# Page attention of a decoder step: the values of four cache pages in one part, directly behind the scores

## The chip, the cores and the metric

The kernel runs on one core of a Trainium2 chip. The metric is the device time of one execution in microseconds (us); lower is better. TensorE does the matrix products and the transpositions, VectorE (DVE) and ScalarE (ACT) copy out of PSUM and do the softmax; GpSimd (POOL), SyncE (SP) and ScalarE issue DMAs. Everything is float32.

## The reference, cut to what matters

One layer of a hybrid decoder is computed for a prompt of 1024 tokens and for 8 samples of 8 new tokens each. The change lies in the attention of the samples over their paged cache: 2048 past tokens in 16 pages of 128 rows, found through a page table, 8 heads of 64.

```
kv_past = cache_fox_kv[page_table, l].reshape(Bd, P, 2, N_FOX_HEADS, HEAD_DIM)
...
k_all = jnp.concatenate([kv_past[:, :, 0], k_new], axis=1)
v_all = jnp.concatenate([kv_past[:, :, 1], v_new], axis=1)
s = jnp.einsum('bqhd,bkhd->bhqk', q, k_all) * (dh ** -0.5)
s = s + c_q.transpose(0, 2, 1)[..., None] - c.transpose(0, 2, 1)[:, :, None, :]
s = jnp.where(mask, s, -inf)
p = softmax(s)
return jnp.einsum('bhqk,bkhd->bqhd', p, v_all)
```

`c` is the running sum of log forget values. After it comes a second page attention of the samples over three dilated windows (13 pages of 128 picked rows, 4 heads each), then gates, projections, a cross-attention and an MLP.

## The kernel before, in words

Each engine has one instruction stream, and its order is written out by `weave`: several generators yield due times (not microseconds), and the one that is due first goes on. `PLAN` holds the stages' due times: the page attention `fox=(869, 1223)`, the gate products `ga=(715, 1010)` and `gb=(1010, 1448)`, `dilprep=(1226, 1228)`, the dilated pages `dil=(1230, 1422)`. On TensorE the page work is woven with the gate products of the prompt (`gates_pe`, L1867 and L1875). A gate unit has 8 + 4 k steps of 352 or 368 columns in the first pass and 8 + 2 in the second; each pass has 24 units. A k step is one product, two matmul records in the trace.

`paged` makes the list of steps for all three page attentions. For the paged cache ("fox") the steps of a sample b are:

- T: the four 128 x 128 transpositions of a page of keys (L1289) into one of two PSUM banks. ScalarE copies out the even pages (L1355), VectorE the odd ones (L1348); page n waits until page n - 2 is copied out.
- S: the scores of a group of four pages, four head pairs in four column tiles of 16 columns (L1305), one slot behind the page that completes the group. One more group, for the 8 new keys, comes one slot behind the sample's first page. VectorE drains each group with the bias added and its maximum taken (L1385).
- M: the maximum over the groups on VectorE (L1390) and one exponential over the row on ScalarE (L1360). TensorE does nothing at M.
- P: transpositions of the probabilities in five blocks (L1314), each copied out to `PT_f` by VectorE (L1400).
- V: the values, 17 blocks in 16 parts of one page each (the last one with the new values), four column tiles again (L1325). They add up in one PSUM bank.
- O: the result scaled (L1407), transposed (L1332) and copied.

Slot i of a sample holds its T of page i; P and V of sample b lie in the slots of sample b + 1, at the offsets in `fox_tail`. All steps of the list get due times in equal steps over `fox`; before, the list has 352 steps.

The pages come by DMA, 256 KB for the keys and 256 KB for the values of one. SyncE loads the keys into four slots (`foxk_sp`, L1500), each when its old page is transposed. ScalarE loads the values into five slots (`foxv_page_act`: page number read at L1514, DMA issued at L1515), each when the part of the page five before is done, in its one stream with its copies. GpSimd spreads the bias rows of each score group with four DMAs (`foxbias_pool`, L1532) into one of two buffers, when this many drains are done:

```
pool.wait_ge(*nth(pg_fox, "drained", bb * 5 + 2 + GG))
```

`dilprep_sp` (L1712) loads a table and then the new dilated keys `kn_d`, 24 DMAs of 8 KB on SyncE's queue (L1721), at a quarter of the `fox` stage. `dilk_sp` and `dilv_sp` load the dilated keys and values. `dilpages_dve` clears `vn_d` and then copies the transposed new keys (L1805, L1809).

## Time and profile before

| | |
|---|---|
| time, median of 3 runs (lowest, highest) | 2754.54 us (2754.12, 2763.18) |
| span of the profiled execution, first to last instruction | 2753.4 us |
| around the span, taken from the median | 1.1 us |
| TensorE matmuls busy | 2717.2 us, 99% |
| VectorE, ScalarE, GpSimd busy | 42%, 19%, 5% |
| mean granted TensorE clock | 0.998 of full |
| HBM traffic | 268.07 MB read, 63.35 MB written, 120 GB/s over the span |
| the page stage on TensorE | about 839 to 1182 us |
| the dilated pages | about 1186 to 1345 us |

The profiled execution's time itself is its span and what lies around it; it is compared with the median of the runs above. Printed durations of matmuls overlap each other: what one takes of TensorE is the difference from its start to the next start. "PEld" is the loading of weights, which lies beside the matmuls. A queue's row such as "SPq" tells from the first issue to the end of the last one.

### The profile page before, as it was taken

How to read it: one execution, taken by the hardware profiler on the slowest of the kernel's cores; microseconds unless marked ns; L12 is line 12 of the kernel's file. 1: busy time of each engine (PE TensorE's matmuls, PEld its weight loads, DVE VectorE, ACT ScalarE, POOL GpSimd, SP SyncE). 2: the span in 40 equal slices, each digit the busy share in tenths (PEclk: the TensorE clock that was granted, in tenths of full speed). 3: DMA queues.
4: the chain of work that ended last, by engine and by line, in shares of the span. 5: the costliest groups of instructions: out<-in, count | busy, mean ns of one | idle time of the engine just before them, and what ended most of it. 6: DMA issues, size and time to landing. Idle time of an engine off the chain costs nothing.

```text
span 2753.4 us, 37659 instructions
## 1 busy us (share of the span) xinstructions
PE 2717.2 (99%) x14274; PEld 1846.9 (67%) x14274; DVE 1151.5 (42%) x2788; ACT 528.6 (19%) x1163; POOL 145.4 (5%) x268
## 2 busy tenths in 40 slices
PE   8999999999999999999999999999999999999998
PEld 7655556767655555456644577546888888888887
DVE  2255543332253233333264023345666666654432
ACT  2233322221201112111002122231212211210002
POOL 1000001020101122100000000000000000000000
PEclk9999999999999999999999999999999999999999
DMA  5000102000116779866512300434435433152201
GB/s 190 22 13 9 59 20 67 32 17 20 46 27 185 210 220 266 248 187 196 217 51 78 136 31 31 147 115 125 146 113 186 145 110 126 46 179 86 80 29 65
DMA packets 207160, 294.48 MB, mean 107 GB/s; under 512 B 20781, under 2 KB 145086, under 8 KB 205942
## 3 DMA queue, kind: packets, MB, share of 16 engines
q1 hardware_dynamic: 148150, 187.76, 21.1%
q10 hardware_dynamic: 42976, 89.26, 10.2%
q0 software_dynamic: 15856, 15.07, 2.3%
q8 instruction: 115, 1.88, 0.3%
q14 instruction: 63, 0.52, 0.1%
HBM read 268.07 MB, written 63.35 MB: 120 GB/s over the span
## 4 chain that ended last, share of the span: by engine, by line
PE 96%; DMA 1%; DVE 1%; issue 1%; SPq 0%; ACTq 0%; ACT 0%; DVEq 0%
PE psum L2523 21%; PE psum L955 11%; PE psum L2904 10%; PE psum L1867 9%; PE psum L531 5%; PE psum L2207 4%; PE psum L1953 4%; PE psum L1289 4%; PE psum L702 3%; PE psum L2054 3%; PE psum L1875 3%; PE psum L718 3%; PE psum L1325 3%; PE psum L1305 2%; PE psum L2181 2%; PE psum L729 2%
## 5 line engine op out<-in xcount | busy, mean ns | idle before, releaser
L2523 PE MATMUL psum<-arena 128*128 128x272 f32 x2464 | 566.6, 393 | 1.2 <-DVE arena L2597 1.2
L2523 PEld LDWEIGHTS psum<-arena 128*128 128x128 f32 x2464 | 469.1, 190 | 98.0 <-issue 1.3
L955 PE MATMUL psum<-arena 128*128 128x512 f32 (+3 forms) x960 | 316.8, 481 | 0.0
L1867 PE MATMUL psum<-arena 128*128 128x368 f32 (+1 forms) x768 | 299.4, 490 | 1.2 <-DVE arena L1809 1.2
L2904 PE MATMUL psum<-arena 128*128 128x256 f32 (+1 forms) x1584 | 288.1, 356 | 0.0
L2904 PEld LDWEIGHTS psum<-arena 128*128 128x128 f32 (+1 forms) x1584 | 252.5, 178 | 34.6 <-issue 3.2
L955 PEld LDWEIGHTS psum<-arena 128*128 128x128 f32 (+1 forms) x960 | 195.0, 250 | 60.7 <-issue 35.1
L778 DVE CUSTOM_DVE_ANT_0 arena<-psum,arena 128x256 f32<-128x256 f32 (+2 forms) x224 | 95.4, 457 | 207.7 <-PE psum L702 207.3
L1867 PEld LDWEIGHTS psum<-arena 128*128 128x128 f32 x768 | 123.7, 191 | 68.5 <-issue 42.9
L2626 DVE TENSOR_TENSOR arena<-arena,psum 128x272 f32<-128x272 f32 (+2 forms) x330 | 111.8, 378 | 112.8 <-PE psum L2523 112.0
L752 ACT ACTIVATE arena<-arena 128x256 f32<-128x256 f32 (+4 forms) x192 | 107.5, 562 | 227.0 <-DVE arena L778 225.5
L1289 PEld LDWEIGHTS psum<-arena 128*128 128x128 f32 x848 | 102.9, 142 | 65.5 <-issue 42.6
L1348 DVE COPY arena<-psum 128x512 f32<-128x512 f32 (+1 forms) x108 | 73.6, 682 | 168.3 <-PE psum L1289 168.2
L531 PE MATMUL psum<-arena 128*128 128x288 f32 (+1 forms) x384 | 137.6, 482 | 0.0
L2647 DVE SCALAR_TENSOR_TENSOR arena<-arena 128x1024 f32<-128x1024 f32 x88 | 113.1, 1285 | 52.6 <-ACT arena L2549 51.1
L1355 ACT ACTIVATE arena<-psum 128x512 f32<-128x512 f32 (+1 forms) x108 | 63.6, 589 | 369.5 <-PE psum L1289 352.3
L1289 PE MATMUL psum<-arena 128*128 128x128 f32 x848 | 130.8, 277 | 3.4 <-DMA arena<-in_cache_fox_kv 3.2
L2547 ACT ACTIVATE arena<-arena 128x1024 f32<-128x1024 f32 x44 | 54.2, 1233 | 399.9 <-DVE arena L2626 399.9
L1953 PE MATMUL psum<-arena 128*128 128x512 f32 x256 | 123.5, 599 | 0.0
L2207 PE MATMUL psum<-arena 128*128 128x288 f32 (+1 forms) x384 | 122.6, 468 | 0.0
L3016 DVE TENSOR_TENSOR arena<-arena,psum 128x256 f32<-128x256 f32 (+1 forms) x128 | 46.6, 401 | 178.9 <-PE psum L2904 178.8
L788 DVE COPY arena<-psum 128x128 f32<-128x128 f32 (+1 forms) x96 | 37.6, 391 | 191.7 <-PE psum L718 191.5
(245 smaller groups left out, 2953.6 us busy)
## 6 DMA issues: line engine op xcount, KB each, us to landing
arena<-in_cache_fox_kv ACTq DMA_DIRECT2D x128, 256.0 KB, 4.2
arena<-in_cache_fox_kv SPq DMA_DIRECT2D x128, 256.0 KB, 4.3
out_win_s<-in_cache_win_kv ACTq DMA_DIRECT2D x8, 4080.0 KB, 15.5
arena<-in_w_up SPq DMA_DIRECT2D x44, 512.0 KB, 6.4
arena<-in_w_down SPq DMA_DIRECT2D x14, 1408.0 KB, 6.3
arena<-in_cache_win_kv SPq DMA_DIRECT2D x16, 1024.0 KB, 7.8
arena<-in_cache_mem_kv SPq DMA_DIRECT2D x16, 1024.0 KB, 6.4
arena<-in_w_in SPq DMA_DIRECT2D x9, 1024.0 KB, 7.8
```

Source lines behind the costliest of these rows:

```text
L531: last = pe.matmul(banks[q % 2][:, 0:cw], w[:, k, j * P:(j + 1) * P], xnT[:, k, c0:c0 + cw], start=(k == 0), stop=(k == KD - 1))
L752: act.activation(p, p, ACT.Exp, scale=-1.0, bias=a["NM"][i], accum_out=a["L"][i]).then_inc(s["expd"], 1)
L778: dve.tensor_tensor_reduce(a["Pb"][i % 4][:, c0:c1], SCORE[h][:, 0:c1 - c0], un["add"](h)[:, c0:c1], 1.0, a["GM"][:, i % 4:i % 4 + 1] if c ...
L955: last = pe.matmul(banks[c0 // 512][p0:p0 + r, 0:n], xn_tile(k, g, t), wD[g][:, k, w0:w0 + n], start=(k == 0), stop=(k == KD - 1))
L1289: last = pe.transpose(a["turn"][n % 2][:, x * P:(x + 1) * P], k, ident)
L1867: last = pe.matmul(banks[0][:, 0:cw], w[:, k, :], xnT[:, k, c0:c0 + cw], start=(k == 0), stop=(k == KD - 1))
L1953: last = pe.matmul(banks[h], lhs(k)[:, t * P:(t + 1) * P], w[h][:, k, :], start=(k == 0), stop=(k == KD - 1))
L2207: last = pe.matmul(banks[u % 2][:, 0:cw], wX[n % 2][:, k, (m % 4) * P:(m % 4 + 1) * P], xnT[:, k, c0:c0 + cw], start=(k == 0), stop=(k == ...
L2523: last = pe.matmul(bank_of(j, x, p), w[:, k, :], r[:, k, Q4 * p:Q4 * p + Q4], start=(k == 0), stop=(k == 3))
L2626: last = dve.tensor_tensor(dst, dst if base is None else view(base), view(bank), ALU.add)
L2647: dve.scalar_tensor_tensor(out=tp, in0=up[:, tap:tap + S], scalar=w, in1=tp, op0=ALU.mult, op1=ALU.add).then_inc(done, 1)
L2904: last = pe.matmul(down_out(u)[p0:p0 + r, 0:n], hT(f)[:, tok + t * P:tok + t * P + r], slot[slots[c]][:, f - fa, c0:c0 + n], start=(f == f ...
```

## The change

Values are taken in four parts of four pages (the last with the new values too), each placed in the slot of a score group and ahead of the other tail work of that slot. On TensorE a score group and a value part that follow each other in the list no longer yield between them, and M is left out of TensorE's list; this holds for all three page attentions. The score group of the new keys moves from behind the first page to behind the last (`new_at`), so it is drained last. The list has 256 steps for the same due span. Values get seven slots instead of five, with one semaphore for every other part; ScalarE loads the pages of a slot when the part that used it is done. The two new slots take the place of `kn_d` and of part of its neighbours; `kn_d` moves onto the first score buffer, so its 24 loads wait until the last probability block of sample 6 is transposed, and `vn_d`, which now overlaps it, is cleared behind the copy of the new keys.

```
--- before.py
+++ after.py
@@ -1212,7 +1212,7 @@
 
 
         def paged(turns, groups, R, kts, s_sb, p_blocks, p_keep, pv, v_split, o_sb, o_blocks, stats, take_out, tail_at, due,
-                  banks_of, add_ready=None, made=False):
+                  banks_of, add_ready=None, made=False, new_at=0):
 
             nt, gl = len(turns(0)), groups(0, None)
             drains = [x for x, g in enumerate(gl) if g["drain"] is not None]
@@ -1239,7 +1239,7 @@
                 sched += [(kind, bb, q) for slot, bb, _, kind, q in tails if slot == n]
                 if b < NB:
                     scores += [("S", b, x) for x in range(len(gl))
-                               if gl[x]["turned"] == i + 1 or (i == 0 and gl[x]["turned"] is None)]
+                               if gl[x]["turned"] == i + 1 or (i == new_at and gl[x]["turned"] is None)]
                     if i == nt - 1:
                         scores.append(("M", b, 0))
             assert not scores
@@ -1277,9 +1277,13 @@
 
         def pages_pe(pe, a, k_ready, v_ready):
             s, z, R = a["s"], a["z"], a["R"]
-            n_d = 0
+            n_d, before = 0, None
             for (what, b, i), t in zip(a["sched"], a["when"]):
-                yield t
+                if what == "M":
+                    continue
+                if before not in ("S", "V") or what not in ("S", "V"):
+                    yield t
+                before = what
                 if what == "T":
                     n = b * a["nt"] + i
                     k_ready(pe, b, i)
@@ -1423,7 +1427,7 @@
             return out
 
 
-        NKR, NVR = 4, 5
+        NKR, NVR = 4, 7
         SF = PAST + P
         s_fox = [take(SF, f0 + 1536 + SF * i) for i in range(2)]
         o_fox = take(P, f0 + 5888)
@@ -1431,7 +1435,7 @@
         biasN = take(SM, f0 + 6080)
         vn_f = take(512, f0 + 6144)
         bias_f = take(1024, f0 + 6656).rearrange("p (g c) -> p g c", g=2)
-        pages = [take(512, f0 + a) for a in (0, 512, 1024, 7680, 8192, 8704, 9216, 9728, 10240)]
+        pages = [take(512, f0 + a) for a in (0, 512, 1024, 7680, 8192, 8704, 9216, 9728, 10240, 27680, 28192)]
         k_fox, v_fox = pages[0:NKR], pages[NKR:]
         PT_f = take((NPG + 1) * 64, f0 + 10752).rearrange("p (n j c) -> p n j c", j=4, c=16)
         biasT = take(PAST, f0 + 11840)
@@ -1447,11 +1451,11 @@
         s_ptab = sem("page_table_loaded")
         fb = sems("foxbias", "vn_in vn_clear suffix cleared summed rows_act rows_dve new_kt new_kept new_in new_turned new_spread")
         s_bias = [sem(f"fox_bias_rows_spread{g}") for g in range(2)]
-        page_in = ring([-(-(NB * NPG - i) // NKR) for i in range(NKR)] + [-(-(NB * NPG - i) // NVR) for i in range(NVR)])
+        page_in = ring([-(-(NB * NPG - i) // NKR) for i in range(NKR)] + [NB * NPG // 2] * 2)
         fk_in, fv_in = page_in[0:NKR], page_in[NKR:]
         kv_pool = I["cache_fox_kv"].rearrange("n l s v h d -> n (l s) v (h d)")
         lf_pool = I["cache_fox_logf"].rearrange("n l s h -> n (l s) h")
-        VP = NPG
+        VP = 4
 
         def ptab_sp(sp):
             sp.dma_start(ptab[:, :], I["page_table"].rearrange("b n -> (b n)").unsqueeze(0)).then_inc(s_ptab, 16)
@@ -1506,13 +1510,13 @@
                     act.wait_ge(s_ptab, 16)
                 before = n - NVR
                 if before >= 0:
-                    yield pg_fox["due_of"][("V", before // NPG, before % NPG)] + 0.1
-                    act.wait_ge(*nth(pg_fox, "mixed", before + 1))
+                    yield pg_fox["due_of"][("V", before // NPG, before % NPG // 4)] + 0.1
+                    act.wait_ge(*nth(pg_fox, "mixed", before // 4 + 1))
                 else:
                     yield at("combine")(1) + 1 + n
                     act.wait_ge(cb["second"], 4)
                 pid = act.value_load(ptab[0:1, n:n + 1], min_val=0, max_val=N_POOL - 1)
-                act.dma_start(v_fox[n % NVR], page_rows(pid, 1)).then_inc(fv_in[n % NVR][0], 16)
+                act.dma_start(v_fox[n % NVR], page_rows(pid, 1)).then_inc(fv_in[n // 4 % 2][0], 16)
 
         def page_rows(pid, v):
 
@@ -1565,14 +1569,14 @@
             if b == 0 and i == VP - 1:
                 eng.wait_ge(fb["vn_in"], 16)
                 eng.wait_ge(fb["vn_clear"], 1)
-            n = b * NPG + i
-            landed(eng, fv_in[n % NVR], n // NVR + 1)
-
-        fox_split = [[p] for p in range(NPG - 1)] + [[NPG - 1, NPG]]
-        fox_tail = [("P", q, 2 + q) for q in range(5)] + [("V", p, 4 + 15 * p // 16) for p in range(NPG)] + [("O", 0, 24)]
+            q = b * VP + i
+            landed(eng, fv_in[q % 2], 4 * (q // 2 + 1))
+
+        fox_split = [list(range(4 * q, 4 * q + (4 if q < 3 else 5))) for q in range(VP)]
+        fox_tail = [("V", q, 4 * (q + 1)) for q in range(VP)] + [("P", q, 2 + q) for q in range(5)] + [("O", 0, 17)]
         pg_fox = paged(fox_turns, fox_groups, P, kts_f, s_fox, NPG + 1, fox_p_keep, fox_pv, fox_split, o_fox, 1, stats_f,
                        pair_out(oTf, 4), fox_tail, PLAN["fox"],
-                       dict(turn=banks[2:4], score=banks[4:6], tail=banks[6], o_ps=banks[7][:, 0:P]), add_ready=fox_add_ready)
+                       dict(turn=banks[2:4], score=banks[4:6], tail=banks[6], o_ps=banks[7][:, 0:P]), add_ready=fox_add_ready, new_at=NPG - 1)
 
         def foxprep_pe(pe):
             now = at("foxprep")
@@ -1662,9 +1666,9 @@
         k_dil = [take(DPG * 256, a).rearrange("p (n c) -> p n c", n=DPG) for a in (f0 + 11840, f0 + 7424)]
         kts_d = [take(1024, a).rearrange("p (j c) -> p j c", j=2) for a in (f0 + 10752, f0 + 15168)]
         PT_mask = take(384, B_at).rearrange("p (n j c) -> p n j c", j=2, c=16)
-        kn_d = take(NG * 256, f0 + 27680).rearrange("p (g c) -> p g c", g=NG)
-        ktn_d = take(NG * 2 * SM, f0 + 28448).rearrange("p (g j c) -> p g j c", g=NG, j=2)
-        tab_d = take(DWID + 192, f0 + 28832)
+        kn_d = take(NG * 256, f0 + 1536).rearrange("p (g c) -> p g c", g=NG)
+        ktn_d = take(NG * 2 * SM, f0 + 28712).rearrange("p (g j c) -> p g j c", g=NG, j=2)
+        tab_d = take(DWID + 192, f0 + 29096)
         win_mask, q_mask = tab_d[0:RD, 0:DWID], tab_d[:, DWID:].rearrange("p (n c) -> p n c", c=16)
         dk_in = [sem(f"window_k_pages_in{i}") for i in range(2)]
         dv_in = sem("window_v_pages_in")
@@ -1715,6 +1719,8 @@
             for g in range(NG):
                 win_stored(sp, g)
             sp.dma_start(tab_d, TAB["win_sample"]).then_inc(dn2["in"], 16)
+            yield pg_fox["due_of"][("P", NB - 2, 4)] + 0.1
+            sp.wait_ge(*nth(pg_fox, "p_turned", 5 * (NB - 1)))
             for g, (w, _) in enumerate(WINS):
                 new = O[f"win{w}_s"][0, :, w - NS:w].rearrange("b s v h d -> b s v (h d)")
                 for bb in range(NB):
@@ -1802,11 +1808,11 @@
             pages_over(dve, pg_fox)
             for i in range(2):
                 dve.memset(s_dil[i][0:RD, DWID:512], 0.0)
-            dve.memset(vn_d, 0.0).then_inc(dn2["cleared"], 1)
             yield at("dilprep")(0.5)
             dve.wait_ge(dn2["in"], DN_IN)
             dve.wait_ge(dn2["turned"], 1)
             dve.tensor_copy(ktn_d.rearrange("p g j c -> p (g j c)"), banks[7][:, 0:NG * 2 * SM]).then_inc(dn2["kept"], 1)
+            dve.memset(vn_d, 0.0).then_inc(dn2["cleared"], 1)
             yield from pages_dve(dve, pg_dil, dil_make)
```

## Rows read from the trace of the kernel before

**Rows 1.** Page, chain that ended last, by engine.
```profile
PE 96%; DMA 1%; DVE 1%; issue 1%; SPq 0%; ACTq 0%; ACT 0%; DVEq 0%
```

**Rows 2.** Windows: us, PE, PEld, DVE, ACT, POOL, clock, DMA share, GB/s.
```profile
1000.00:1100.00 100.00, 100.00 (x839) 53.87 (x839) 37.40 (x91) 21.62 (x35) 24.26 (x44) 1.00 0.88 258
...
1154.80:1186.50 31.70, 26.75 (x240) 12.11 (x240) 8.71 (x23) 3.16 (x5) 0.00 (x0) 0.95 0.68 220
```

**Rows 3.** Timeline of PE, 1014 to 1021: start, us, instructions.
```profile
1015.01 0.78 PE L1867 MATMUL psum<-arena 128*128 128x368 f32 x2
1015.63 0.60 PE L1314 MATMUL psum<-arena 128*128 128x128 f32 x4
1016.07 0.60 PE L1289 MATMUL psum<-arena 128*128 128x128 f32 x4
1016.50 0.78 PE L1867 MATMUL psum<-arena 128*128 128x368 f32 x2
1017.22 1.05 PE L1305 MATMUL psum<-arena 128*16 128x512 f32 x8
1018.20 0.89 PE L1867 MATMUL psum<-arena 128*128 128x368 f32 x2
```

**Rows 4.** Timeline of PE, 1029 to 1046.
```profile
1036.93 1.05 PE L1305 MATMUL psum<-arena 128*16 128x512 f32 x8
1037.80 0.40 PE L1325 MATMUL psum<-arena 128*16 128x128 f32 x8
1038.13 0.89 PE L1867 MATMUL psum<-arena 128*128 128x368 f32 x2
1038.85 0.60 PE L1289 MATMUL psum<-arena 128*128 128x128 f32 x4
1039.38 0.41 PE L1325 MATMUL psum<-arena 128*16 128x128 f32 x8
1039.72 0.89 PE L1867 MATMUL psum<-arena 128*128 128x368 f32 x2
```

**Rows 5.** Timeline of PE: first and last of 155 runs.
```profile
841.22 0.30 PE L1305 MATMUL psum<-arena 128*16 128x64 f32 x8
...
1180.49 0.85 PE L1325 MATMUL psum<-arena 128*16 128x128 f32 x24
```

**Rows 6.** Timeline of ACT: issues of its queue and a copy.
```profile
1038.93 1.95 ACTq L1515 DMA_DIRECT2D arena<-in_cache_fox_kv  x2
1041.08 0.60 ACT L1355 ACTIVATE arena<-psum 128x512 f32<-128x512 f32 x1 [3.51 <-PE psum L1289]
...
1168.17 8.25 ACTq L1515 DMA_DIRECT2D arena<-in_cache_fox_kv  x8
```

**Rows 7.** Page loads, 1000 to 1148: keys (L1500), then values (L1515).
```profile
DMA to landing us min/median/max: 2.9/4.6/7.4
...
DMA to landing us min/median/max: 3.3/4.6/8.6
```

**Rows 8.** DMA issues, 1000 to 1100: bias rows; KB, median landing.
```profile
arena<-arena POOLq DMA_DIRECT2D x44, 32.0 KB, 3.6
```

**Rows 9.** Timeline, 936 to 958: the 24 loads; a page behind.
```profile
940.23 9.46 SPq L1721 DMA_DIRECT2D arena<-out_win_s  x24
...
953.65 0.66 PE L1289 MATMUL psum<-arena 128*128 128x128 f32 x4 [0.28 <-DMA arena<-in_cache_fox_kv]
```

**Rows 10.** Windows: a low-clock spell (columns as in rows 2).
```profile
1176.60:1180.50 3.90, 3.86 (x21) 1.29 (x22) 0.00 (x0) 0.00 (x0) 0.00 (x0) 0.56 0.33 115
```

**Rows 11.** Value loads (L1515), 1157 to 1161, then 1168 to 1177.
```profile
DMA to landing us min/median/max: 7.2/7.2/7.8
...
DMA to landing us min/median/max: 2.8/3.1/3.9
```

**Rows 12.** Timeline of PE, 1172 to 1182: value page waits.
```profile
1173.63 0.41 PE L1325 MATMUL psum<-arena 128*16 128x128 f32 x8 [1.01 <-DMA arena<-in_cache_fox_kv]
1173.97 0.89 PE L1867 MATMUL psum<-arena 128*128 128x368 f32 x2
...
1176.64 0.59 PE L1325 MATMUL psum<-arena 128*16 128x128 f32 x8 [1.44 <-DMA arena<-in_cache_fox_kv]
```

More of the change, by code:

```diff
@@ L1214, in paged @@
         def paged(turns, groups, R, kts, s_sb, p_blocks, p_keep, pv, v_split, o_sb, o_blocks, stats, take_out, tail_at, due,
-                  banks_of, add_ready=None, made=False):
+                  banks_of, add_ready=None, made=False, new_at=0):
             nt, gl = len(turns(0)), groups(0, None)
@@ L1241, in paged @@
                     scores += [("S", b, x) for x in range(len(gl))
-                               if gl[x]["turned"] == i + 1 or (i == 0 and gl[x]["turned"] is None)]
+                               if gl[x]["turned"] == i + 1 or (i == new_at and gl[x]["turned"] is None)]
                     if i == nt - 1:
@@ L1279, in pages_pe @@
             s, z, R = a["s"], a["z"], a["R"]
-            n_d = 0
+            n_d, before = 0, None
             for (what, b, i), t in zip(a["sched"], a["when"]):
-                yield t
+                if what == "M":
+                    continue
+                if before not in ("S", "V") or what not in ("S", "V"):
+                    yield t
+                before = what
                 if what == "T":
@@ L1423, in pair_out @@
             return out
-        NKR, NVR = 4, 5
+        NKR, NVR = 4, 7
         SF = PAST + P
@@ L1433, in build @@
         bias_f = take(1024, f0 + 6656).rearrange("p (g c) -> p g c", g=2)
-        pages = [take(512, f0 + a) for a in (0, 512, 1024, 7680, 8192, 8704, 9216, 9728, 10240)]
+        pages = [take(512, f0 + a) for a in (0, 512, 1024, 7680, 8192, 8704, 9216, 9728, 10240, 27680, 28192)]
         k_fox, v_fox = pages[0:NKR], pages[NKR:]
@@ L1449, in build @@
         s_bias = [sem(f"fox_bias_rows_spread{g}") for g in range(2)]
-        page_in = ring([-(-(NB * NPG - i) // NKR) for i in range(NKR)] + [-(-(NB * NPG - i) // NVR) for i in range(NVR)])
+        page_in = ring([-(-(NB * NPG - i) // NKR) for i in range(NKR)] + [NB * NPG // 2] * 2)
         fk_in, fv_in = page_in[0:NKR], page_in[NKR:]
@@ L1453, in build @@
         lf_pool = I["cache_fox_logf"].rearrange("n l s h -> n (l s) h")
-        VP = NPG
+        VP = 4
         def ptab_sp(sp):
@@ L1508, in foxv_page_act @@
                 if before >= 0:
-                    yield pg_fox["due_of"][("V", before // NPG, before % NPG)] + 0.1
-                    act.wait_ge(*nth(pg_fox, "mixed", before + 1))
+                    yield pg_fox["due_of"][("V", before // NPG, before % NPG // 4)] + 0.1
+                    act.wait_ge(*nth(pg_fox, "mixed", before // 4 + 1))
                 else:
@@ L1567, in fox_v_ready @@
                 eng.wait_ge(fb["vn_clear"], 1)
-            n = b * NPG + i
-            landed(eng, fv_in[n % NVR], n // NVR + 1)
-        fox_split = [[p] for p in range(NPG - 1)] + [[NPG - 1, NPG]]
-        fox_tail = [("P", q, 2 + q) for q in range(5)] + [("V", p, 4 + 15 * p // 16) for p in range(NPG)] + [("O", 0, 24)]
+            q = b * VP + i
+            landed(eng, fv_in[q % 2], 4 * (q // 2 + 1))
+        fox_split = [list(range(4 * q, 4 * q + (4 if q < 3 else 5))) for q in range(VP)]
+        fox_tail = [("V", q, 4 * (q + 1)) for q in range(VP)] + [("P", q, 2 + q) for q in range(5)] + [("O", 0, 17)]
         pg_fox = paged(fox_turns, fox_groups, P, kts_f, s_fox, NPG + 1, fox_p_keep, fox_pv, fox_split, o_fox, 1, stats_f,
                        pair_out(oTf, 4), fox_tail, PLAN["fox"],
-                       dict(turn=banks[2:4], score=banks[4:6], tail=banks[6], o_ps=banks[7][:, 0:P]), add_ready=fox_add_ready)
+                       dict(turn=banks[2:4], score=banks[4:6], tail=banks[6], o_ps=banks[7][:, 0:P]), add_ready=fox_add_ready, new_at=NPG - 1)
         def foxprep_pe(pe):
@@ L1664, in build @@
         PT_mask = take(384, B_at).rearrange("p (n j c) -> p n j c", j=2, c=16)
-        kn_d = take(NG * 256, f0 + 27680).rearrange("p (g c) -> p g c", g=NG)
-        ktn_d = take(NG * 2 * SM, f0 + 28448).rearrange("p (g j c) -> p g j c", g=NG, j=2)
-        tab_d = take(DWID + 192, f0 + 28832)
+        kn_d = take(NG * 256, f0 + 1536).rearrange("p (g c) -> p g c", g=NG)
+        ktn_d = take(NG * 2 * SM, f0 + 28712).rearrange("p (g j c) -> p g j c", g=NG, j=2)
+        tab_d = take(DWID + 192, f0 + 29096)
         win_mask, q_mask = tab_d[0:RD, 0:DWID], tab_d[:, DWID:].rearrange("p (n c) -> p n c", c=16)
@@ L1717, in dilprep_sp @@
             sp.dma_start(tab_d, TAB["win_sample"]).then_inc(dn2["in"], 16)
+            yield pg_fox["due_of"][("P", NB - 2, 4)] + 0.1
+            sp.wait_ge(*nth(pg_fox, "p_turned", 5 * (NB - 1)))
             for g, (w, _) in enumerate(WINS):
@@ L1804, in dilpages_dve @@
                 dve.memset(s_dil[i][0:RD, DWID:512], 0.0)
-            dve.memset(vn_d, 0.0).then_inc(dn2["cleared"], 1)
             yield at("dilprep")(0.5)
@@ L1809, in dilpages_dve @@
             dve.tensor_copy(ktn_d.rearrange("p g j c -> p (g j c)"), banks[7][:, 0:NG * 2 * SM]).then_inc(dn2["kept"], 1)
+            dve.memset(vn_d, 0.0).then_inc(dn2["cleared"], 1)
             yield from pages_dve(dve, pg_dil, dil_make)
```

2 lines of the change are left out of this document (1 added, 1 removed).

## The prediction

> **What bounds the kernel now.** The chain of waits comes first: 96% of it is TensorE [rows 1]. So an edit is worth what it takes out of TensorE's own stream, less what it makes that stream wait. Next the windows: at 1000 to 1100 TensorE is busy for all 100 us at the full granted clock (1.0, the 2.4 GHz level), while the DMA engines are at 0.88 of their time [rows 2]. TensorE is the limit there, with little DMA room. At the end of the page stage (1154.8 to 1186.5) it is idle 31.70 - 26.75 = 4.95 us, and the clock is 0.95 [rows 2]. Last the timeline, read by start-to-start times, since the printed durations overlap.
>
> **What a value run costs.** Scores (L1305) and values (L1325) use 16 weight columns; transpositions and gate products use 128. I call an unbroken stretch of the first kind a run. A pair of gate products (one k step) takes 1015.63 - 1015.01 = 0.62, a page's transpositions 0.43, the same pair ahead of a run 0.72, a score group 0.98 [rows 3]. A page's values alone take 0.34, but score group plus values take 0.87 + 0.33 = 1.20, so the page itself is 0.22. The pair behind a run takes 0.72, transpositions ahead of one 0.53 [rows 4]. One run thus costs 0.10 in the work ahead, 0.34 - 0.22 = 0.12 inside, and 0.10 behind, somewhat less where a page's transpositions follow: I take 0.30 us beyond its matmuls (at most 0.32; at least 0.22, if what follows a run were not held up at all).
>
> **Part 1: fewer runs.** The old page stage has 128 value parts and 40 score groups. Along the timeline they form 155 runs, the first at 841.22, the last at 1180.49 [rows 5]. In the new schedule every value part of samples 0 to 6 stands directly behind a score group, the new keys' group directly behind score group 3, and with no yield between them nothing gets in. Merging both lists with the gate products by due time (254 k steps in either) gives 34 runs. 121 runs x 0.30 = 36.3 us gained. The same rule in `pages_pe` acts on the dilated pages: the merge gives 51 runs before and 40 after, 11 x 0.30 = 3.3 us. In the cross-attention pages no score meets a value part: 0. Skipping "M" on TensorE removes nothing but a yield: 0.
>
> The matmuls of values, scores and transpositions stay the same; only their order moves. No DMA is added.
>
> **Part 2: ScalarE holds its page copies behind four loads.** ScalarE issues the value loads and copies out every even transposed page, in one static order. A load starts 0.73 us after its values end (1037.80 + 0.40 to 1038.93), eight in a row take 8.25 us, so one each 1.13; a copy takes 0.60 [rows 4, 6]. Before, one load stood between copies. Now four stand together: the copy of the first even page behind value part q is done at 0.73 + 3 x 1.13 + 0.60 and a third of a microsecond for the last issue, 5.1 us. The page two later needs that bank. The list now has 256 entries for 354 due units (1.38 each) instead of 352 (1.01). While the first gate pass runs there are some seven k steps between a value part and that page: 7 x 0.62 + 3 x 0.43 = 5.6, covered. In the second pass gate products are sparser (438 units for 240 k steps, against 295 for 288). Behind parts 1 and 2, where no probability transpositions help, three or four remain: 0.1 + 3 or 4 x 0.62 + 3 x 0.43 = 3.25 or 3.9. The stall is 1.8 or 1.2. Counted in the list: two at 1.8, six at 1.2, and one of 1.0 before score group 3 of the last sample, 11.8 us. Behind parts 0 and 3 there are 6.5 us or more, covered. ScalarE's sequencer issues loads while the exponential runs, so that adds nothing.
>
> **Part 3: page transfers.** Keys keep four slots. A short group is 4 x 0.62 + 4 x 0.43 + 0.87 + 4 x 0.22 + 0.30 = 6.3 us of TensorE work plus the stall of part 2, so a slot has some 7.1 between two uses; to the issue I allow SyncE ScalarE's 0.73, and landing takes 4.6 (median) to 7.4 [rows 7]. So most arrive and the late tail does not: 2.5 us in all (bounds 0 and 9 x 1.1 = 10, if landings rise to the 7.4). Values: the last page of part q+1 can only be loaded once part q is done, but has 0.73 + 4.6 = 5.3 against about 6.7: mostly hidden. The bias refill of GpSimd counts drains by `bb * 5 + 2 + GG`; with the new keys' drain moved from first to last the same number comes one group later. Its four issues and 3.6 of landing [rows 8] fit into the 7.5 us of a stalled short group; taken as 0, at worst 1 us a sample.
>
> **Part 4: the new dilated keys.** Twenty-four small issues hold SyncE for 9.46 us. Before, they stood where pages were over 2 us apart, and TensorE waited 0.28 [rows 9]. Now they stand behind the last probability transposition of sample 6, that is, between the key loads of pages 122 and 123. Page 123 lands at 1.3 (to that wait) + 9.5 + 0.8 + 2.9 (the shortest landing) = 14.5 us behind the transpositions of page 118; TensorE has 7 x 0.62 + 5 x 0.43 + 0.87 + 0.88 + 0.30 = 8.5 of work. Stall 6.0, plus a spell of half clock (1.2 GHz): 3.9 us at 0.56 lose 1.7 [rows 10]. Together 7.7 us (bounds 5 and 10). ScalarE's value loads go on meanwhile. Nothing else is queued on SyncE but the last five key loads, and those follow 1.1 apart.
>
> **Part 5: the end of the stage.** Behind the last score groups nothing but ten k steps and the probability transpositions remain, and the last three value parts stand next to each other. Each of the last two waits for a page loaded only after the part before: 0.73 + 3.1 [rows 11] less what overlaps = 3.6 each. The first part of sample 7 needs a page issued just behind part 3 of sample 6, together with the first dilated keys; there landings took 7.2 [rows 11]: 1.2 + 7.2 less 5.1 of work = 3.3. With two or three half-clock spells (4 us), closer transpositions (1) and the small waits that stay (0.7) this makes 16.2. Before it was 4.95 idle and 1.7 for the clock, of which 1.2 was the wait for the copy behind the `vn_d` memset: 5.4 without that. Net loss 10.8 (bounds 5 and 14). Moving the memset behind the copy gives back part of the 1.2, and the first queries are made later: +0.5.
>
> **The sum.** 36.3 + 3.3 + 0.5 = 40.1 gained; 11.8 + 2.5 + 7.7 + 10.8 = 32.8 lost; net 7.3. The profiled span is 2753.4 us and the median of the runs 2754.54, 1.1 more for what lies around it. 2754.5 - 7.3 = 2747.2, or 2747.
>
> **The clock.** A half-clock spell follows waits of 1.01 and 1.44 us with one value part between them [rows 10, 12]; it costs 1.7 us. I count it for the long waits of parts 4 and 5 alone, because the first of these two waits had none behind it: the values there still took their usual 0.34. If all nine short groups of part 2 brought one, it would be 9 x 1.7 = 15 us more, 2762: rival (d). The Trainium skill ("TensorE: Matmul & The Clock Gate", section "HAM oscillation") says just that of loops in which each short piece of compute is followed by a wait for a DMA: every next piece starts at the low clock.
>
> **Rivals.** (a) *Forecast, 0.45*: the saved runs are mostly handed back as waits; own range 2740 to 2760. (b) *The waits are mostly hidden, 0.31*: ScalarE's loads or the copies run quicker than 1.13 and 0.60, or gate products lie so that the page two later comes later, and transfers land early. Parts 2 and 3 fall away: 2754.5 - 40.1 + 18.5 = 2733. For it: ScalarE is busy only 21.62 us of the 100 [rows 2]. Against: the order is static and the hold is issue time. (c) *Slower, 0.15*: the value ring itself becomes the bound. A part's last page has 5.4 us of natural cover; if its landing, now in bursts of four, is 7.2 as where two streams met [rows 11], each of the nine short groups waits 0.73 + 7.2 - 5.4 = 2.5 instead of 1.3, 11 us more, and at such waits the clock halves each time, 15 more: 2747 + 26 = 2773. It decides from landings of about 6.5 on. DMA at 0.88 before, with 8 pages in a group of 7 us instead of 9, speaks for it; three of four pages loaded a group ahead speak against. (d) *A low-clock spell behind each short group, 0.09*: 2762, as above; waits of 1.2 to 1.8 us every 8 us lie between the one that had no spell and the pair that had one.
>
> **How the numbers follow.** 0.5% is 13.8 us, about what this kernel's runs can tell from no change. (a) and (d) lie within it; (b) is faster but for 0.02 at its slow edge, (c) is slower, and (a) and (d) send 0.01 and 0.01 over the bounds: faster 0.30, same 0.54, slower 0.16. The range takes in (b) with a margin of 4, (a) and (d), and leaves out (c): 2729 to 2768.
>
> **What the profile after would show.** Value parts as runs of 32 matmuls directly behind L1305, 34 runs in the stage, and k steps of 0.62 between pages (part 1). ScalarE: four L1515 issues in 3.8 us and page waits `PE L1289 <- ACT L1355` of 1.2 to 1.8 twice a sample from sample 3 on (part 2). One wait of some 6 us for a key page near the end, behind 24 issues of SyncE (part 4). Three waits of over 3 us for value pages in the last 30 us, clock below 0.9 (part 5). The forecast is wrong if the nine waits are absent, if they come with the low clock, or if runs cost less than 0.30 once the gate products stand together.

## The result, and the profile after

The changed kernel takes 2776.64 us (median of five runs, 2774.89 to 2779.29), the kernel before, run on the same chip, 2754.54 us (2753.5 to 2766.7): a ratio of 1.0073 [1.0059, 1.0087]. It is 22 us slower, where I forecast 7 us faster, and it lies outside my range of 2729 to 2768. The profiled execution has a span of 2774.8 us.

In the changed file the lines are: transposition of keys L1293, scores L1309, probability transposition L1318, values L1329; copies out by VectorE L1352 and by ScalarE L1359, exponential L1364, drain L1389; gate products L1873 and L1881, their sigmoid on ScalarE L1909; issues of the values L1519, of the keys L1504, of the new dilated keys L1727, of gate weights on ScalarE's queue L1847 and L1848, of the bias rows L1536.

The page of the changed kernel, chain that ended last, by engine; in [rows 1] TensorE had 96% and ScalarE's queue (ACTq) 0%:

```profile
PE 92%; ACTq 3%; DMA 1%; issue 1%; DVE 1%; ACT 1%; SPq 0%; POOL 0%; DVEq 0%; POOLq 0%
```

Windows of the changed kernel (columns as in [rows 2]):

```profile
838.00:1000.00 162.00, 152.85 (x1114) 96.69 (x1112) 46.42 (x107) 30.19 (x54) 30.91 (x56) 0.99 0.75 215
1000.00:1100.00 100.00, 82.53 (x711) 52.33 (x711) 32.38 (x81) 20.05 (x33) 22.05 (x40) 0.93 0.76 217
...
1154.00:1208.00 54.00, 37.78 (x329) 21.86 (x329) 12.38 (x32) 5.69 (x10) 2.20 (x4) 0.78 0.62 191
```

From 1000 to 1100 TensorE was never idle before [rows 2]; now 17.5 us of it are idle and the clock is at 0.93, while the DMA engines have become emptier (0.76, was 0.88). So the stage has not become short of transfer bandwidth. Whom TensorE waits for is in its waits from 830 to 1250 (who ended the wait: us in total, times, longest), first of the kernel before:

```profile
PE psum L1289 <- DMA arena<-in_cache_fox_kv: 3.2, 4, 1.5
PE psum L1325 <- DMA arena<-in_cache_fox_kv: 3.1, 3, 1.4
```

and of the changed kernel:

```profile
PE psum L1293 <- ACT arena L1359: 25.9, 13, 3.8
PE psum L1329 <- DMA arena<-in_cache_fox_kv: 8.4, 3, 3.4
PE psum L1873 <- ACT arena L1909: 7.1, 5, 3.1
PE psum L1293 <- DMA arena<-in_cache_fox_kv: 4.8, 5, 3.0
PE psum L1309 <- issue: 1.6, 1, 1.6
```

With the smaller ones (1.2 and 0.6 before; 1.2, 0.9 and 0.6 after) 8.1 us of waits have become 50.5. The clock adds to it: its loss in a window is (1 - clock) x length, 1.6 + 7.0 + 11.9 = 20.5 us over the three windows above (between 1100 and 1154 it is 1.00). The trace's record of the clock has the half-clock stretches themselves: five of 3.4 us at 990, 1014, 1035, 1045 and 1059, one of 10.2 at 1154, 3.4 at 1181 and 10.2 at 1192. They add up to 40.8 us, and half of that, 20.4, is lost at most. Before it was two of 3.4 us, 3.4 lost. The table further down uses this half.

The saved runs are there: the timeline has 34 of them in the page stage and 40 in the dilated pages, as forecast. A short group of the changed kernel, timeline of TensorE:

```profile
1067.76 0.79 PE L1873 MATMUL psum<-arena 128*128 128x368 f32 x2
1068.38 0.27 PE L1318 MATMUL psum<-arena 128*128 128x128 f32 x1
...
1069.98 0.78 PE L1881 MATMUL psum<-arena 128*128 128x368 f32 x2
1070.70 1.05 PE L1309 MATMUL psum<-arena 128*16 128x512 f32 x8
1071.57 1.06 PE L1329 MATMUL psum<-arena 128*16 128x128 f32 x32
1072.55 0.89 PE L1881 MATMUL psum<-arena 128*128 128x368 f32 x2
1073.27 0.78 PE L1873 MATMUL psum<-arena 128*128 128x368 f32 x2
```

From start to start: a k step 1067.76 to 1068.38, 0.62; ahead of the run 0.72, the scores 0.87, the values of four pages 0.98, the pair behind 0.72. By my prices it should be 0.72, 0.87, 0.12 + 4 x 0.22 = 1.00 and 0.72 [rows 3, 4].

And so is the hold of ScalarE, but longer than I priced it. Timeline of ScalarE with its queue, changed kernel, and below it two lines of TensorE from the same stretch:

```profile
1038.10 4.84 ACTq L1519 DMA_DIRECT2D arena<-in_cache_fox_kv  x4
1042.97 0.45 ACTq L1847 DMA_DIRECT2D arena<-in_w_in  x1
1043.45 1.11 ACTq L1848 DMA_DIRECT2D arena<-in_w_br_dil  x1
1044.66 0.60 ACT L1359 ACTIVATE arena<-psum 128x512 f32<-128x512 f32 x1 [9.79 <-issue]
```

```profile
1035.42 1.95 PE L1329 MATMUL psum<-arena 128*16 128x128 f32 x32
...
1045.40 1.09 PE L1293 MATMUL psum<-arena 128*128 128x128 f32 x4 [3.84 <-ACT arena L1359]
```

The value part ends at 1037.37, the copy at 1045.26: 7.9 us, where I had 5.1. The first issue starts after the 0.73 that I took. The four take 4.84 instead of 3 x 1.13 + 0.34 = 3.73. Then two weight loads, which I had left out, take another 1.6. The page's transposition stands still for 3.84 us, and its four matmuls then run at the half clock (1.2 GHz), in 1.09 us, where four took 0.60 [rows 3].

### The profile page after: what moved, and what is told of

Read it like the earlier page. It is cut to its first block, busy times and chain, and to the rows that moved or that the text cites. A ratio compares the mean times of both kernels' runs of the same rounds, so it can differ in the third digit from the quotient of the medians.

```text
span 2774.8 us, 37563 instructions
## 1 busy us (share of the span) xinstructions
PE 2696.1 (97%) x14274; PEld 1872.1 (67%) x14274; DVE 1150.4 (41%) x2788; ACT 528.6 (19%) x1163; POOL 145.4 (5%) x268
## 4 chain that ended last, share of the span: by engine, by line
PE 92%; ACTq 3%; DMA 1%; issue 1%; DVE 1%; ACT 1%; SPq 0%; POOL 0%; DVEq 0%; POOLq 0%
PE psum L2529 20%; PE psum L955 11%; PE psum L2910 10%; PE psum L1873 7%; PE psum L531 5%; PE psum L2213 4%; PE psum L1959 4%; PE psum L702 3%; PE psum L2060 3%; PE psum L718 3%; PE psum L1293 3%; PE psum L1881 2%; PE psum L1309 2%; PE psum L1329 2%; PE psum L2187 2%; PE psum L729 2%
## 5 line engine op out<-in xcount | busy, mean ns | idle before, releaser
L2529 PEld LDWEIGHTS psum<-arena 128*128 128x128 f32 x2464 | 469.3, 191 | 98.0 <-issue 1.3
L1873 PE MATMUL psum<-arena 128*128 128x368 f32 (+1 forms) x768 | 288.4, 486 | 7.7 <-ACT arena L1909 7.1
L1873 PEld LDWEIGHTS psum<-arena 128*128 128x128 f32 x768 | 129.6, 193 | 61.4 <-issue 17.4
L1293 PEld LDWEIGHTS psum<-arena 128*128 128x128 f32 x848 | 104.6, 143 | 97.1 <-issue 72.1
L1293 PE MATMUL psum<-arena 128*128 128x128 f32 x848 | 130.1, 278 | 30.9 <-ACT arena L1359 25.9
L1359 ACT ACTIVATE arena<-psum 128x512 f32<-128x512 f32 (+1 forms) x108 | 63.6, 589 | 383.0 <-PE psum L1293 285.9
L1352 DVE COPY arena<-psum 128x512 f32<-128x512 f32 (+1 forms) x108 | 73.5, 681 | 144.4 <-PE psum L1293 144.4
```

Of the source, the lines that this page charges most:

```text
L1293: last = pe.transpose(a["turn"][n % 2][:, x * P:(x + 1) * P], k, ident)
L1873: last = pe.matmul(banks[0][:, 0:cw], w[:, k, :], xnT[:, k, c0:c0 + cw], start=(k == 0), stop=(k == KD - 1))
L2529: last = pe.matmul(bank_of(j, x, p), w[:, k, :], r[:, k, Q4 * p:Q4 * p + Q4], start=(k == 0), stop=(k == 3))
```

## The experiments

For each run: its median and that of the kernel before on the same chip, the difference D, TensorE's waits from 830 to 1250 and half the length of the half-clock stretches there. "Work" is D less what waits and clock have grown over the 8.1 + 3.4 of the kernel before, that is, the work saved. If part 1 is right, it is -39.6 for every kernel with the new order and the joining. Kernels are compared by their D. D is a difference of medians, but waits and clock are those of one profiled execution, which in e1, e2, e6 and e9 was 2 to 4 us slower than the median and in e4 3 us faster. So the last two columns stay within the profiled executions: "stage" is the time from the first gate product (L1867) to the first matmul behind the gates and pages (L2054), 650.4 us in the kernel before, and "by stage" the same subtraction made with it in place of D. What lies outside the stage is 2102.4 to 2104.2 us in all twelve kernels.

| run | us | before | ratio | D | waits | clock | work | stage | by stage |
|---|---|---|---|---|---|---|---|---|---|
| the change | 2776.6 | 2754.5 | 1.0073 [1.0059, 1.0087] | +22.1 | 50.5 | 20.4 | -37.3 | 671.2 | -38.6 |
| e1 | 2759.5 | 2756.8 | 1.0008 [0.9998, 1.0019] | +2.7 | 40.2 | 20.4 | -46.4 | 658.8 | -40.7 |
| e2 | 2772.7 | 2756.8 | 1.0050 [1.0032, 1.0067] | +15.9 | 50.5 | 20.4 | -43.5 | 670.1 | -39.7 |
| e3 | 2804.0 | 2753.5 | 1.0188 [1.0172, 1.0204] | +50.5 | 61.5 | 25.5 | -25.0 | 699.3 | -26.6 |
| e4 | 2751.1 | 2756.8 | 0.9973 [0.9961, 0.9984] | -5.8 | 11.3 | 5.1 | -10.6 | 643.0 | -12.3 |
| e5 | 2751.9 | 2753.5 | 0.9995 [0.9982, 1.0009] | -1.6 | 32.6 | 15.3 | -38.0 | 647.7 | -39.1 |
| e6 | 2767.9 | 2756.8 | 1.0036 [1.0025, 1.0047] | +11.1 | 46.7 | 20.4 | -44.5 | 665.5 | -40.5 |
| e7 | 2743.7 | 2753.5 | 0.9966 [0.9952, 0.9979] | -9.8 | 28.2 | 5.1 | -31.5 | 637.0 | -35.2 |
| e8 | 2730.9 | 2753.5 | 0.9924 [0.9909, 0.9938] | -22.6 | 19.2 | 5.1 | -35.4 | 625.9 | -37.3 |
| e9 | 2764.1 | 2756.3 | 1.0020 [1.0010, 1.0030] | +7.8 | 44.7 | 17.0 | -42.4 | 660.5 | -40.1 |
| e10 | 2756.9 | 2756.3 | 0.9999 [0.9987, 1.0011] | +0.6 | 36.7 | 15.3 | -39.9 | 653.1 | -37.8 |

**e1: the value loads apart.** Is it the four issues in a row that hold the copies?

```
-                    yield pg_fox["due_of"][("V", before // NPG, before % NPG // 4)] + 0.1
+                    apart = 1.4 if before < NPG * (NB - 1) else 0
+                    yield pg_fox["due_of"][("V", ...)] + 0.1 + apart * (before % 4)
```

> Only the order of ScalarE's stream changes: the four value loads behind a part are 1.4 due units apart, so that page copies get between them (not for the last sample). Theory A, the hold: the changed kernel's 25.9 us of TensorE waiting for ScalarE's page copies and 7.7 for its gate sigmoids fall below 8 together, and the five low-clock spells between 990 and 1062 (8.5 us lost) go with them; 2740 to 2750 us. Theory B, the page transfers or the ring of seven value slots are the bound: the time stays above 2770 and the waits turn up as waits for value or key pages.

D is 19.4 us less than the changed kernel's, but at 2759.5 us it misses the 2740 to 2750 of theory A and is not below the kernel before. Waits of TensorE, e1, two rows:

```profile
PE psum L1293 <- DMA arena<-in_cache_fox_kv: 16.7, 14, 8.0
...
PE psum L1293 <- ACT arena L1359: 4.4, 2, 2.5
```

The wait for the copy went from 25.9 to 4.4, as the theory of the hold says. The time did not go where I had put it, since other waits grew. One is behind the 24 loads: 7.96 us for one key page at 1150, with 10.2 us of half clock. The other thirteen waits for key pages are 8.7 us, where the changed kernel had 1.4 besides the two behind its loads. And VectorE waits for the bias rows. Its waits from 838 to 1200, first e1, then the changed kernel:

```profile
DVE arena L1389 <- DMA arena<-arena: 46.7, 13, 5.7
```

```profile
DVE arena L1389 <- DMA arena<-arena: 13.0, 4, 4.0
```

**e2: the 24 new-key loads later** (the changed kernel, with these loads behind the last key load, so that no key load waits for them: part 4 of the prediction).

```
-            yield pg_fox["due_of"][("P", NB - 2, 4)] + 0.1
+            yield pg_fox["due_of"][("M", NB - 1, 0)] + 0.2
```

> Only the 24 loads of the new dilated keys move on SyncE, from behind page 122's key load to behind the last key load and the first dilated pages. Theory A with my part 4: the waits for key pages of 3.0 and 0.4 us near 1157 go, and with them up to half of the 10.2 us at the low clock (5 us lost): 2768 to 2773. Theory B: the wait near 1157 is for bandwidth and stays, 2776.

6.2 us less, but the intervals of the two ratios overlap. The key-page waits fell from 4.8 to 1.3. The sum of all waits stayed at 50.5, since those for sigmoids rose from 7.1 to 9.6 and others by 1.0. Most of the rise lies ahead of 1145 (31.4 to 34.3), where nothing was changed. From 1145 on the waits fell from 19.2 to 16.2 and the clock's share by 1.7 us. Timeline of SyncE's queue, of the change:

```profile
1145.53 10.38 SPq L1727 DMA_DIRECT2D arena<-out_win_s  x24
```

So part 4 was a cost, 4.7 us in the traces and 6.2 in the medians, where I had 7.7; how large exactly these runs can't tell.

**e3: the changed kernel with a yield before every step again.** That undoes the joining alone; the values stay in four parts behind the scores.

```
-                if before not in ("S", "V") or what not in ("S", "V"):
-                    yield t
+                yield t
```

> The changed kernel with a yield ahead of every step of TensorE's list again (M too), so gate products get between scores and values: merged by due time 67 runs instead of 34 in the page stage and 51 instead of 40 in the dilated one. 44 x 0.30 = 13 us more if nothing hides them: 2790. In the stretches in which TensorE waits for ScalarE anyway they are free, so about half: 2780 to 2786. If runs cost nothing: 2777.

28.4 us more, so 2804.0, where I had expected 2780 to 2786. The page stage has 67 runs instead of 34 and the dilated pages 51 instead of 40, so 44 x 0.30 = 13.2 us more. The work column says 37.3 - 25.0 = 12.3, the one by stage 12.0. The waits grew by 11.0 and the clock by 5.1 besides. The copies' wait in e3, 25.9 in the change (the sigmoids' is 10.9, was 7.1):

```profile
PE psum L1292 <- ACT arena L1358: 31.9, 15, 4.0
```

Perhaps the shift in the order moved gate products away from where they hid the hold; that is not shown.

**e4: the kernel before with the joining rule alone** (one-page value parts, five slots).

```
-                yield t
+                if what == "M":
+                    continue
+                if before not in ("S", "V") or what not in ("S", "V"):
+                    yield t
+                before = what
```

> The kernel before with nothing but the new rule of TensorE's list: no yield between scores and values, M left out. Values by single pages, five slots, loads and new keys as before. Merged by due time the page stage has 125 runs instead of 155, the dilated pages 40 instead of 51. Run price 0.30 us: 41 x 0.30 = 12.3 us, 2742. If the DMA engines at 0.88 allow no faster pages, or a run costs nothing, 2752 to 2755.

It is faster than before, by 5.8 us; I had expected 2742, 12.3 less. There are 30 and 11 fewer runs, 12.3 us by my price; the work column has 10.6, the one by stage 12.3. Waits and clock took back 4.9: 6.2 more from 1145 on, 1.3 less ahead of it. TensorE waits for value pages, e4 (3.1 before):

```profile
PE psum L1329 <- DMA arena<-in_cache_fox_kv: 6.3, 9, 1.3
```

**e5: e1 and e2 together.**

> e1 and e2 together: value loads 1.4 due units apart, and the 24 loads of new dilated keys behind the last key load. Theory A (issue time in static queues): the wait of 8.0 us for a key page near 1151 in e1 goes and with it at least half of the 10.2 us of low clock beside it, so 10 to 13 us below e1: 2746 to 2750 us, faster than before by 7 or so. Rival: with both queues free the transfers themselves take the time back as key and value page waits, 2755 or more.

4.3 us below e1 by D (the intervals overlap), where I had expected 10 to 13. In the profiled executions it is 11.1 by the stage; e1's was the slowest of its ten. From 1145 on the waits are 13.4, in e1 20.2, and the clock's share is 3.4 us less: the wait of 8 us behind the 24 loads is gone, as expected. The key-page waits are 9.6 us in all now, 16.7 in e1.

**e6: each value load a quarter as wide** (128 of its 512 columns). It keeps the number of issues and their place, and takes three quarters of the values' bytes out of the queues. That tells the hold (issue time) from rival (c) (transfer time).

```
-                act.dma_start(v_fox[n % NVR], page_rows(pid, 1)).then_inc(...)
+                act.dma_start(v_fox[n % NVR][:, 0:128], page_rows(pid, 1)[:, 0:128]).then_inc(...)
```

> The changed kernel with value loads of 128 of the 512 columns, so a quarter of the bytes with the same issues in the same places; the values of the other columns are not loaded, so the result of the page attention is not the reference's. Theory A: ScalarE holds its copies by issue time, so the waits for copies stay above 18 of 25.9 us; only the long issues and the three waits for value pages at the end (8.4 us) shrink: 2758 to 2769. Theory B, transfers: the waits in the middle go too, 2742 or less.

The values' landing from 838 to 1154 fell to a median of 3.3 us (4.7 in the change), and the copies' wait stayed:

```profile
PE psum L1293 <- ACT arena L1359: 24.8, 13, 3.5
```

Rival (c) is refuted, though its time was the nearest to the result. In the changed kernel itself the values wait for a page only three times, all after 1180. The smaller loads still saved 11.0 us by D, 5.7 in the stage; 3.8 of it are waits, the rest is not accounted for.

**e7: the end of the stage.** e5, and the values of pages 119 to 122 go into the four key slots once the last keys are transposed, so that the last two value parts need not wait for each other's slots. (The load takes its slot and its semaphore from two small functions.)

```
+        def v_slot(n):
+            return v_fox[n % NVR] if n < 119 else k_fox[n - 119] if n < 123 else v_fox[(n - 4) % NVR]
...
+                if 119 <= n < 123:
+                    yield pg_fox["due_of"][("V", NB - 2, 3)] + 0.1 + 1.4 * (n - 115)
+                    act.wait_ge(*nth(pg_fox, "turned", 124 + n - 119 + 1))
```

> e5, and at the end four value pages of the last sample (119 to 122) go into the four key slots, which are free by then, and the last five into the value slots that part 0 and part 1 of the last sample leave; two more semaphores. Theory: the last two waits for value pages (3.4 and 3.4 us in e1) shrink to under 1 and under 3, and half of the 10.2 us spell there goes: 8 to 11 us below e5, 2736 to 2741. Rival: the end of the stage is bound by its probability chain and by the dilated keys' 1.6 MB, so the waits move to VectorE or to the dilated pages and less than 3 us is gained.

8.2 us less than e5. The values' waits went from 9.6 to 5.3 (two are left, the longest 2.7, where I had expected one under 1). The clock's share went from 15.3 to 5.1. Half of that lies ahead of 1145, where the change of e7 does not reach and the waits stayed as they were (19.1 and 19.5), so that half is no effect of e7.

**e8: e7, and the bias rows one drain earlier.** In e7 VectorE still waits 13 times at the drain for the bias rows, 42.4 us in all.

```
-                    pool.wait_ge(*nth(pg_fox, "drained", bb * 5 + 2 + GG))
+                    pool.wait_ge(*nth(pg_fox, "drained", bb * 5 + 1 + GG))
```

> e7 with the count that GpSimd waits for before it refills a bias buffer lowered by one, as the new order of drains allows. If the late refill costs nothing, as I took it: same as e7 within 2 us. If it held VectorE and through it the banks: 3 to 8 us below e7.

12.9 us less than e7, where I had expected 3 to 8; at 2730.9 us it is the fastest kernel here, 22.6 us or 0.76% faster than the kernel before. How a late bias reaches TensorE is seen in e7 from 991 to 1008, a line of GpSimd's timeline, one of VectorE's and three of ScalarE's with its queue:

```profile
991.39 2.20 POOL L1546 DMA_DIRECT2D arena<-arena  x4 [5.74 <-DVE arena L1389]
...
998.90 0.69 DVE L1389 CUSTOM_DVE_ANT_0 arena<-psum,arena 128x512 f32<-128x512 f32 x1 [2.89 <-DMA arena<-arena]
...
1000.84 2.06 ACT L1364 ACTIVATE arena<-arena 128x2112 f32<-128x2112 f32 x1 [3.88 <-DVE arena L1394]
...
1004.36 3.14 ACTq L1529 DMA_DIRECT2D arena<-in_cache_fox_kv  x2
1007.60 0.60 ACT L1359 ACTIVATE arena<-psum 128x512 f32<-128x512 f32 x1 [4.62 <-issue]
```

The four spreads start only after a drain; the group's drain stands 2.89 us for them; the row's maximum and the exponential follow it; one value load is issued while the exponential runs, and the next two only behind it, with 3.14 us for both; and the copy behind them ends at 1008.20, for which TensorE waits 2.41 us. The links up to the exponential are releases that the profile shows; that the exponential is what holds the two loads is my reading of their order. In e8 no drain waits for a DMA, and TensorE's waits are, the first three:

```profile
PE psum L1293 <- DMA arena<-in_cache_fox_kv: 10.6, 12, 1.7
PE psum L1329 <- DMA arena<-in_cache_fox_kv: 4.7, 2, 2.5
PE psum L1293 <- ACT arena L1359: 1.6, 2, 1.3
```

The copies are gone from the top; now the four key slots come first.

**e9: the changed kernel with e8's one line alone.** Does the late bias cost anything while the hold of four issues is still there?

> The changed kernel with GpSimd's count for the bias refill lowered by one and nothing else. In the changed kernel only 4 of 32 score groups were drained more than 0.5 us behind their scores, 5 us in sum, against 13 and 21 us in e7, so if the hold of ScalarE masks it: 2772 to 2777. If the late bias is a cause of its own of the slowdown: 2763 to 2768, 10 to 13 us less, as in e8 against e7.

14.3 us less than the changed kernel, 10.7 by the stage, so the late bias is a cause of its own. In the changed kernel only four drains wait (13.0 us in all, above), but the copies' wait went to 22.5 and the sigmoids' to 5.2 without them, and the half-clock stretches of 990 and 1014 are not there.

```profile
PE psum L1293 <- ACT arena L1359: 22.5, 12, 3.3
```

**e10: e8 with the value loads in a row again.**

```
-                    apart = 1.4 if before < NPG * (NB - 1) else 0
+                    apart = 0
```

> e8 with the four value loads behind a part issued together again (before the last sample), all else as e8: late new keys, key slots for the last pages, the right bias count. If the hold is the largest term: 17 us or more above e8 (as e1 against the changed kernel), so 2748 to 2758, with waits for ScalarE's copies of over 20 us again. If the hold only mattered together with the other three: within 6 us of e8.

23.2 us more than e8, all the gain that e8 had over the kernel before. The copies' wait is back:

```profile
PE psum L1293 <- ACT arena L1359: 22.4, 12, 3.8
```

From the changed kernel to e8, in the order made: spreading 19.4, late keys 4.3, the end 8.2, bias 12.9, together 44.8 us. Taken singly, spreading is 23.2 at the end of that order, late keys 6.2 and the bias line 14.3 at its beginning. These pairs differ by 3.8, 1.9 and 1.4 us, about as much as chips do: the kernel before has medians from 2753.5 to 2756.8.

## Why the prediction was wrong, point by point

**Part 1, right.** In the work column the nine kernels with 34 and 40 runs have -31.5 to -46.4, on average -39.9; I forecast 36.3 + 3.3 = 39.6. By the stage, which leaves out what one execution differs from the median, they lie closer together: -35.2 to -40.7, on average -38.8. e3 agrees with 12.0 to 12.3 for 13.2, e4 with 10.6 to 12.3 for 12.3. The end of the stage is seen in the first matmuls behind it, kernel before, then changed kernel:

```profile
1366.62 3.67 PE L2054 MATMUL psum<-arena 128*128 128x512 f32 x8 [0.83 <-issue]
```

```profile
1386.22 4.07 PE L2060 MATMUL psum<-arena 128*128 128x512 f32 x5 [0.83 <-issue]
```

The first gate product starts at 716.21 and 715.00. The stage is 20.8 us longer, with (50.5 + 20.4) - (8.1 + 3.4) = 59.4 us more lost in it: 38.6 gained.

**Part 2, the step that failed: "11.8 us".** The mechanism is the one I named, its size is not. In the changed kernel ScalarE's copies and sigmoids cost 25.9 + 7.1 + 0.6 = 33.6 us, and the five half-clock stretches from 990 to 1059 up to another 8.5: 42 us. Four terms were short.

(1) The hold of 5.1 us. At 983, changed kernel, timeline of TensorE, and below it ScalarE from the same stretch:

```profile
982.35 1.06 PE L1329 MATMUL psum<-arena 128*16 128x128 f32 x32
983.33 0.86 PE L1873 MATMUL psum<-arena 128*128 128x352 f32 x2
...
984.46 0.76 PE L1873 MATMUL psum<-arena 128*128 128x352 f32 x2
...
985.50 0.76 PE L1873 MATMUL psum<-arena 128*128 128x352 f32 x2
986.09 0.60 PE L1293 MATMUL psum<-arena 128*128 128x128 f32 x4
990.27 1.09 PE L1293 MATMUL psum<-arena 128*128 128x128 f32 x4 [3.58 <-ACT arena L1359]
```

```profile
984.42 5.01 ACTq L1519 DMA_DIRECT2D arena<-in_cache_fox_kv  x4
989.53 0.60 ACT L1359 ACTIVATE arena<-psum 128x512 f32<-128x512 f32 x1 [8.46 <-issue]
```

This is in the second gate pass: each pass has half of L1873's 768 matmul records, and the second half begins at 980.8. There are three k steps, and the cover from the values' end (983.41) to where the page would start (990.27 - 3.58 = 986.69) is 3.3 us, as I forecast for this pass (3.25). The hold to the copy's end is 6.7 us. It was 7.9 at 1037, where two weight loads follow. The four issues of 3.73 took 3.5 to 5.0, and I had let nothing but loads of values stand there, though weight loads and the gate units' sigmoids use the same stream. Behind eight value parts of the second pass three or four k steps stand, the number that I counted, and the eight waits there are 19.4 us for my 10.8. The one before score group 3 of the last sample is 1.6 for 1.0 (the row "issue" above: ScalarE's copy ends at 1171.25, the scores start at 1171.34).

(2) "Behind parts 0 and 3 there are 6.5 us or more, covered", because "ScalarE's sequencer issues loads while the exponential runs, so that adds nothing". At 1004, changed kernel, ScalarE:

```profile
1004.96 2.06 ACT L1364 ACTIVATE arena<-arena 128x2112 f32<-128x2112 f32 x1 [3.03 <-DVE arena L1394]
...
1008.35 3.70 ACTq L1519 DMA_DIRECT2D arena<-in_cache_fox_kv  x3
```

One load was issued while the exponential ran (at 1005.85), the three others behind it. The part's values end at 1004.07 and the next copy at 1012.75, a hold of 8.7 us, and 6.8 of cover did not hide it: TensorE waits 1.99 us at 1012.89. At 1100.33, with the weight loads behind the values' loads, it waits 2.50. In the first gate pass the cover held: from 845 to 980 there are two such waits, 0.46 and 0.51 us.

(3) The waits for sigmoids, 7.7 us: those who wait are gate products, a wait that I did not have at all.

(4) The clock behind these waits, up to 8.5 us, which I did not count. The trace of before had a warning that I passed over: a single wait of 1.50 us with half clock right behind it, 845.7 to 849.1, four transpositions in 1.11 us instead of 0.60.

```profile
845.61 1.11 PE L1289 MATMUL psum<-arena 128*128 128x128 f32 x4 [1.50 <-DMA arena<-in_cache_fox_kv]
```

e1 and e10 show that the issues standing together are the cause of the copies' waits (19.4 and 23.2 us), e6 that their transfers are not.

**Part 3, a second step that failed: the bias refill "taken as 0".** I had the facts (one group later, four issues, 3.6 us of landing) and compared them with a stalled short group of 7.5 us. The group behind it is drained when its scores are done, and what the drain holds is VectorE's one stream, and with it the row's maximum and the exponential. Measured: 14.3 us, above the 1 us a sample that I had called the worst. The key transfers look right in the changed kernel, 1.4 us outside the 24 loads for my 2.5, but that was luck: the other waits gave them time. With the hold gone they are 8.7 us in e1 and 10.6 in e8, about the upper bound that I gave.

**Part 4, right in kind.** The wait is 2.96 + 0.43 = 3.4 us instead of 6.0, because TensorE had just stood 3.06 us for a sigmoid and the loads went on meanwhile; in e1, without that, it is 7.96. The half clock of 10.2 us begins at 1154.1, behind the sigmoid's wait and ahead of the key page's. In e2, with the sigmoid's wait alone, 3.4 us of it are left. So the loads' share is up to 3.4 instead of 1.7. Together 6.8 for 7.7. Timeline of TensorE, changed kernel, this and the end:

```profile
1154.94 1.60 PE L1873 MATMUL psum<-arena 128*128 128x368 f32 x2 [3.06 <-ACT arena L1909]
1159.50 1.12 PE L1293 MATMUL psum<-arena 128*128 128x128 f32 x4 [2.96 <-DMA arena<-in_cache_fox_kv]
...
1192.51 1.91 PE L1329 MATMUL psum<-arena 128*16 128x128 f32 x32 [3.44 <-DMA arena<-in_cache_fox_kv]
...
1197.73 2.33 PE L1329 MATMUL psum<-arena 128*16 128x128 f32 x40 [3.32 <-DMA arena<-in_cache_fox_kv]
```

**Part 5, right in its sum, partly by luck.** The three value waits are 1.64, 3.44 and 3.32 (forecast 3.3, 3.6, 3.6), the probability copies 1.2 and the clock up to 6.8: 16.4, forecast 16.2. The first wait is half of its forecast, and the clock, which I had at 4, makes up for it.

**The rivals.** (b) is out: the waits were not hidden. (c) gave 2773, near the result for the wrong reason: e6 takes three quarters of the bytes away and the wait stays. (d) was half right: the low clock came behind some short groups, not all. Of the ten waits of 1.4 to 2.6 us in the stage, three had a half-clock stretch behind them (1.99, 1.87, 1.64); all seven of 2.6 or more had one, or lay in one. I gave (a) to (d) as alternatives. What happened is Part 2 grown, with (d) on top and the bias beside it. My range did not hold such a sum, since each rival changed one term or two and left the others as they were.

The Trainium skill ("TensorE: Matmul & The Clock Gate", section "HAM oscillation") has every piece of compute start at the low clock in a loop whose waits for a DMA are about 3 to 5 us. The trace agrees for the long waits above, and it has three of 1.64 to 1.99 us besides.

What stays open: whether a fifth key slot would remove the 10.6 us of key waits that e8 has left. It was not tried. That the half-clock stretches are caused by the waits was not tested by itself; the kernels with the fewest waits (e4, e8, e7) have the least (5.1 us lost), but e7 against e5 shows that nearly equal waits can come with different amounts.

## What to carry to other kernels

An engine that both copies for the critical engine and issues loads must be costed by its whole stream in the stretch after the trigger: every issue, every other function in it, at the issue times seen when the queues are full. Joining small matmul groups was worth its price; what it cost was the bunching of everything released by the larger group, and spreading that out again (a due time for each load) was a small edit. A wait can be hidden by another: those for key pages came out only when the hold was gone. When a step of a group changes its place in an order, look for every count on that group's semaphore in other engines: here one `+ 2` that should have become `+ 1` was worth 13 to 14 us, half a per cent.

## What was not expected of the hardware

An issue of ScalarE's queue that usually takes 1.13 us from one to the next took longer in places, though the DMA engines were not full: at 1038 four took 4.84 us, and in e7 at 1004 two took 3.14. One weight load of the changed kernel, at 981, took 2.28 us to issue.

Cutting the values' bytes to a quarter (e6) did not make it shorter: four in 4.22 us there. Twenty-four small issues of SyncE took 10.38 us in the change, 9.46 before [rows 9], 11.64 in e1 and 8.61 in e2.
